# Keys and values of the memory: from the second block's layers to the first block, by way of DRAM

## The reference

```python
def mixer_layer(x, mem, layer_idx, g_norm, w_in, lam_p, w_mem_kv, g_mem, ...):
    h = rmsnorm(x, g_norm)
    z = jnp.einsum('bsd,dn->bsn', h, w_in)            # w_in: 1024 x 13312
    ...
    mem_n = rmsnorm(mem, g_mem)
    kv = jnp.einsum('bmd,dn->bmn', mem_n, w_mem_kv).reshape(B, mem.shape[1], 2, MEM_HEADS, MEM_HEAD_DIM)
    o_m = memory_attention(mq, kv[:, :, 0], kv[:, :, 1])
    ...
    return x + jnp.einsum('bsd,de->bse', merged, w_out)

def second_block(x, mem, ...):
    for l in range(DEPTH):                            # DEPTH = 2
        x = mixer_layer(x, mem, l, g_norm[l], w_in[l], ..., w_mem_kv[l], g_mem[l], ...)
    return rmsnorm(x, g_final)
```

## Time and profile before

| | us |
|---|---|
| median of 3 runs | 2410.48 |
| lowest, highest | 2403.91, 2410.59 |
| profiled execution, its own time | 2403.4 |
| its span | 2401.7 |
| PE busy | 2059.7 (86%) |
| VectorE, ScalarE, POOL busy | 480.6, 377.8, 14.3 |
| moved by DMA | 588.20 MB, 245 GB/s over the span |

### The profile page before, as it was taken

One profiled execution on the slowest core, in us unless ns is written; L12 is line 12 of the kernel. 1 busy time (PEld: TensorE's weight loads), 2 busy tenths in 40 slices (PEclk: granted clock), 3 DMA queues, 4 the chain that ended last, 5 costly groups with the idle time before them and its releaser, 6 DMA issues.

```text
span 2401.7 us, 35672 instructions
## 1 busy us (share of the span) xinstructions
PE 2059.7 (86%) x15302; PEld 1405.7 (59%) x15302; DVE 480.6 (20%) x970; ACT 377.8 (16%) x840; POOL 14.3 (1%) x21
## 2 busy tenths in 40 slices
PE   7868988878738998888739999999985999999997
PEld 4636666666536666666527487455543848745543
DVE  3531111111251111111220023221211002222112
ACT  2501111001011110000020122221102012221111
POOL 0000000000000000000000000000000000000000
PEclk9878999989978998899969999999997999999999
DMA  9156999999976999999754433523315443353330
GB/s 355 49 219 239 421 421 420 420 419 420 394 305 246 420 420 420 420 420 420 310 189 166 149 120 126 189 86 128 140 38 209 140 166 115 106 192 105 123 123 26
DMA packets 140628, 588.20 MB, mean 245 GB/s; under 512 B 13680, under 2 KB 14960, under 8 KB 90928
## 3 DMA queue, kind: packets, MB, share of 16 engines
q1 hardware_dynamic: 134368, 565.13, 59.7%
q0 software_dynamic: 6096, 20.72, 2.4%
HBM read 579.51 MB, written 6.29 MB: 244 GB/s over the span
## 4 chain that ended last, share of the span: by engine, by line
issue 52%; PE 40%; DVE 4%; ACT 2%; DMA 1%; DVEq 0%; SPq 0%; POOL 0%; ACTq 0%; POOLq 0%
PE ps L441 22%; PE ps L430 10%; PE ps L387 2%; PE ps L436 2%; PE ps L413 2%; PE ps L359 1%; ACT arena L507 1%; DVE arena L632 1%; DVE tiny L636 1%; DVE arena L656 1%; DMA arena<-in_mem_dram 1%; ACT arena L491 1%; DVE arena L655 0%; DMA pos_i<-in_positions_dram 0%; DMA arena<-in_diff_lambda_dram 0%
## 5 line engine op out<-in xcount | busy, mean ns | idle before, releaser
L441 PE MATMUL ps<-ring,xT 128*128 128x512 f32 x960 | 418.3, 593 | 0.0
L925 PE MATMUL ps<-ring,xT 128*32 128x128 f32 x8192 | 278.4, 293 | 87.7 <-DMA ring<-in_moe_w_dram 80.6
L925 PEld LDWEIGHTS ps<-ring,xT 128*32 128x32 f32 x8192 | 251.4, 115 | 140.3 <-DMA ring<-in_moe_w_dram 87.1
L430 PE MATMUL ps<-xT,ring 128*128 128x256 f32 x1408 | 309.7, 380 | 0.0
L441 PEld LDWEIGHTS ps<-ring,xT 128*128 128x128 f32 x960 | 180.7, 190 | 214.4 <-issue 213.7
L430 PEld LDWEIGHTS ps<-xT,ring 128*128 128x128 f32 x1408 | 265.4, 190 | 39.9 <-issue 4.9
L907 PE MATMUL ps<-arena,x_tm 128*128 128x128 f32 x1024 | 257.4, 410 | 9.8 <-DVE arena L1433 8.5
L907 PEld LDWEIGHTS ps<-arena,x_tm 128*128 128x128 f32 x1024 | 248.9, 334 | 18.6 <-issue 9.7
L958 PE MATMUL ps<-arena 128*32 128x512 f32 x768 | 141.9, 700 | 31.7 <-DVE arena L1448 31.7
L441 PE MATMUL ps<-ring,arena 128*128 128x512 f32 x320 | 141.5, 599 | 1.8 <-ACT arena L491 1.8
L359 PE MATMUL ps<-consts,arena 128*128 128x128 f32 x352 | 56.3, 299 | 86.4 <-DVEq L618 70.7
(11 more groups left out here) (239 smaller groups left out, 1448.5 us busy)
## 6 DMA issues: line engine op xcount, KB each, us to landing
ring<-in_moe_w_dram SPq DMA_DIRECT2D x288, 1024.0 KB, 24.4
ring<-in_w_in_dram SPq DMA_DIRECT2D x52, 2048.0 KB, 8.2
arena<-in_moe_w_dram SPq DMA_DIRECT2D x96, 1024.0 KB, 26.1
ring<-in_w_mem_kv_dram SPq DMA_DIRECT2D x4, 2048.0 KB, 9.3
ring<-in_w_br_diff_dram SPq DMA_DIRECT2D x4, 2048.0 KB, 7.9
ring<-in_w_out_dram SPq DMA_DIRECT2D x4, 2048.0 KB, 8.0
ring<-gap_bias POOLq DMA_DIRECT2D x4, 1536.0 KB, 10.1
gap_bias<-arena POOLq DMA_DIRECT2D x1, 5120.0 KB, 53.5
```

Source lines behind the costliest of these rows:

```text
L430: m = nc.tensor.matmul(bank[:, u * T:(u + 1) * T], w[:, k, f * P:(f + 1) * P], x_[:, k, :], start=(k == 0), stop=(k == KD - 1))
L441: m = nc.tensor.matmul(bank, x_[:, k, half * P:(half + 1) * P], w[:, k, :], start=(k == 0), stop=(k == KD - 1))
L925: m = nc.tensor.matmul(ps[SL * q:SL * q + SL, g % 2, s * P:(s + 1) * P], xs[:, g % 2, k, s * SL:(s + 1) * SL], w[:, c0:c0 + 2 * P - 1:2], ...
```

## The change

The keys and values of the memory no longer are made in the second block. In the first block:

- SP loads `mem` and both layers' `g_mem` at the start, and the memory's weights of layer 0 (4 MB) into slots 0 and 1, where experts 0 and 1 were loaded before; expert 0 is loaded after the second keys piece, expert 1 after the last values piece, expert 2 when both stores are done.
- ScalarE squares `mem`, VectorE scales it by the root, PE turns it, VectorE copies it to `memT`. POOL multiplies it by `g_mem` of layer 0 and of layer 1 and stores the second product in DRAM (`memT_dram`).
- PE makes the keys in two pieces (`mem_keys`, 16 matmuls of 256 columns each) and the values in two (`mem_values`, 8 of 512 columns each). Layer 0: keys before attention, keys and values after the output product, values behind the logits. Layer 1: both keys pieces ahead of the pooling products, with `memT` read back, values behind these, values behind the logits.
- ScalarE (VectorE for the very first) copies each piece to SBUF, and POOL stores keys and values in `mk_dram` and `mv_dram`.
- Around the pooling layer SP loads the memory's weights of layer 1 and expert 0, then the pooling's vectors, and experts 1 to 3 at later points. The scaling of `acc` by ScalarE moves ahead of the exponentials.

In the second block the two chunks, the squares, scaling, turns and copies of `mem` are gone, and POOL reads keys and values back behind `g_norm`. The diff, cut to its core:

```diff
-    plan = [(("mem_kv", 0), None, None), (("mem_kv", 1), None, None)]
-    plan += [(w[c], None, None) for c in range(8)]
+    plan = [(w[c], None, None) for c in range(8)]
...
+        mem_tm, memT = places(ring, 2 * UPW, 3 * UPW, (TT, D), (KD, T))
+        mem_sq = carve(arena, 8448, TT, D)
+        memT_of = [carve(ring, 2 * UPW, KD, T), carve(ring, 3 * UPW, KD, T)]
+        mk_w = [carve(ring, 0, KD, CW), carve(ring, UPW, KD, CW)]
+        mv_w = [carve(ring, UPW, KD, CW), carve(ring, 2 * UPW, KD, CW)]
+        mk_new = [carve(ring, s * UPW + KD * T, MH, T) for s in (2, 3)]
+        mv_new = [carve(ring, s * UPW + KD * T + MH * T, TT, MH * HD) for s in (2, 3)]
...
-                for src in (mem_tm, h_tm):
-                    turn_tiles([[src[:, t, k::KD] for k in (2 * c, 2 * c + 1) for t in range(TT)] for c in range(4)])
-                pe.wait_ge(sem("turn_read"), l * NTURN + 8)
+                turn_tiles([[h_tm[:, t, k::KD] for k in (2 * c, 2 * c + 1) for t in range(TT)] for c in range(4)])
+                pe.wait_ge(sem("turn_read"), l * NTURN + 4)
...
-                for n, src in enumerate((x_tm, mem_tm)):
-                    for t in range(TT):
-                        i = nc.scalar.activation(PT3.rearrange("p a b -> p (a b)")[:, 0:D], src[:, t, :], ACT.Square,
-                                                 accum_out=ssq4[:, 2 * n + t:2 * n + t + 1])
-                        i.then_inc(sem("ssq_each"), 1)
-                        act.wait_ge(sem("ssq_each"), l * 4 + 2 * n + t + 1)
+                for t in range(TT):
+                    i = nc.scalar.activation(PT3.rearrange("p a b -> p (a b)")[:, 0:D], x_tm[:, t, :], ACT.Square,
+                                             accum_out=ssq4[:, t:t + 1])
+                    i.then_inc(sem("ssq_each"), 1)
+                    act.wait_ge(sem("ssq_each"), l * TT + t + 1)
                 act.sem_inc(sem("ssq_ready2"), 1)
-                act_root2(act, l * 2 + 1, 4)
+                act_root2(act, l * 2 + 1, TT)
...
-                    pool.dma_start(mem_tm, a["mem"][0].rearrange("(t p) d -> p t d", p=P)).then_inc(sem("mem_in"), 16)
                     pool.dma_start(g_x, a["g_norm"][bass.ds(l, 1), :].rearrange("a d -> (a d)").partition_broadcast(P)
                                    ).then_inc(sem("g_in"), 16)
-                    pool.dma_start(g_m, a["g_mem"][bass.ds(l, 1), :].rearrange("a d -> (a d)").partition_broadcast(P)
-                                   ).then_inc(sem("g_in"), 16)
+                    pool.dma_start(mkT, mk_dram[bass.ds(l, 1)].rearrange("a p (h t) -> (a p) h t", h=MH)).then_inc(
+                        sem("mkv_in"), 16)
+                    pool.dma_start(mv, mv_dram[bass.ds(l, 1)].rearrange("a p (t n) -> (a p) t n", t=TT)).then_inc(
+                        sem("mkv_in"), 16)
...
+            sp.dma_start(mem_tm, a["mem"][0].rearrange("(t p) d -> p t d", p=P)).then_inc(sem("mem_in"), 16)
+            sp.dma_start(gm, a["g_mem"].rearrange("l (p k) -> p l k", k=KD), allow_slow_non_contiguous=True).then_inc(
+                sem("gm_in"), 16)
             sp.dma_start(wuq, a["mla_w_uq"][0].rearrange("(k p) n -> p k n", p=P)).then_inc(sem("wuq_in"), 16)
             sp.dma_start(wukv, a["mla_w_ukv"][0]).then_inc(sem("wukv_in"), 16)
             sp.dma_start(wo, a["mla_w_o"][0].rearrange("(k p) n -> p k n", p=P)).then_inc(sem("wo_in"), 16)
-            for e in range(3):
-                load_up(sp, 0, e)
+            load_mem_w(sp, 0)
...
+            sp.wait_ge(sem("mkv_ps"), 2)
+            load_up(sp, 0, 0)
             sp.wait_ge(sem("ln_done"), 1)
             load_ln(sp, 0, 1, gain, shift)
+            sp.wait_ge(sem("mkv_ps"), 4)
+            load_up(sp, 0, 1)
             sp.wait_ge(sem("A_ready"), 1)
             load_route(sp, 1)
+            sp.wait_ge(sem("mk_out"), 16)
+            sp.wait_ge(sem("mv_out"), 16)
+            load_up(sp, 0, 2)
             load_experts(sp, 0, 0)
...
+            sp.wait_ge(sem("up"), done * NE + NE - 1)
+            load_mem_w(sp, 1)
+            sp.wait_ge(sem("up"), done * NE + NE)
+            sp.wait_ge(sem("memT_out"), 16)
+            sp.dma_start(memT_of[1], memT_dram.rearrange("p (k t) -> p k t", k=KD)).then_inc(sem("memT_in"), 16)
+            load_up(sp, 1, 0)
             sp.wait_ge(sem("down"), done * (2 * GROUPS) + 2 * GROUPS - 2)
             for dst_, src_ in ((pb, a["pool_b"]), (psc, a["pool_scale"])):
                 sp.dma_start(dst_, src_[0].partition_broadcast(P)).then_inc(sem("pool_in"), 16)
             load_ln(sp, 1, 0, pool_gain, pool_shift)
-            for e in range(4):
-                sp.wait_ge(sem("up"), done * NE + NE - 3 + e)
-                load_up(sp, 1, e)
             sp.wait_ge(sem("down"), nsw * (2 * GROUPS))
             for e in range(6):
                 load_down(sp, 1, e)
+            sp.wait_ge(sem("mkv_ps"), 6)
+            load_up(sp, 1, 1)
             sp.wait_ge(sem("ln_done"), 2)
             load_ln(sp, 1, 1, gain, shift)
             sp.wait_ge(sem("ln_done"), 3)
             load_up(sp, 1, 4)
             load_down(sp, 1, 6)
             load_down(sp, 1, 7)
+            sp.wait_ge(sem("mkv_ps"), 8)
+            load_up(sp, 1, 2)
+            sp.wait_ge(sem("mk_out"), 32)
+            sp.wait_ge(sem("mv_out"), 32)
+            load_up(sp, 1, 3)
             load_experts(sp, 1, nsw)
...
+        def mem_keys(pe, layer, half, bank):
+            if half == 0:
+                pe.wait_ge(sem(f"mkv_w0"), 16 * (layer + 1))
+            for u in range(2):
+                f = 2 * half + u
+                for k in range(KD):
+                    i = nc.tensor.matmul(ps[:, bank, u * T:(u + 1) * T], mk_w[layer][:, k, f * P:(f + 1) * P],
+                                         memT_of[layer][:, k, :], start=(k == 0), stop=(k == KD - 1))
+            i.then_inc(sem("mkv_ps"), 1)
+
+        def mem_values(pe, layer, half, bank):
+            if half == 0:
+                pe.wait_ge(sem(f"mkv_w1"), 16 * (layer + 1))
+            for k in range(KD):
+                i = nc.tensor.matmul(ps[:, bank, :], memT_of[layer][:, k, half * P:(half + 1) * P],
+                                     mv_w[layer][:, k, :], start=(k == 0), stop=(k == KD - 1))
+            i.then_inc(sem("mkv_ps"), 1)
+
         def transpose_x(pe, n):
 
+            if n == 1:
+                pe.wait_ge(sem("mkv_taken"), 3)
+            if n == 3:
+                pe.wait_ge(sem("mkv_taken"), 7)
...
+            mem_values(pe, layer, 1, 3)
             pe.wait_ge(sem("A_ready"), layer + 1)
...
+            pe.wait_ge(sem("mem_normed"), 1)
+            for c in range(4):
+                for u in range(2):
+                    for t in range(TT):
+                        i = nc.tensor.transpose(ps[:, 4 + c, u * T + t * P:u * T + (t + 1) * P],
+                                                mem_tm[:, t, 2 * c + u::KD], ident)
+                i.then_inc(sem("memT_ps"), 1)
...
+            pe.wait_ge(sem("k_ready"), 8)
+            pe.wait_ge(sem("memT0_ready"), 1)
+            mem_keys(pe, 0, 0, 3)
...
+            pe.wait_ge(sem("mkv_taken"), 1)
+            mem_keys(pe, 0, 1, 6)
+            mem_values(pe, 0, 0, 7)
...
+            pe.wait_ge(sem("memT_in"), 16)
+            for half in range(2):
+                mem_keys(pe, 1, half, half)
...
+            pe.wait_ge(sem("pool_ready"), 4)
+            mem_values(pe, 1, 0, 7)
...
+            act.wait_ge(sem("ln_done"), 2 * layer + 1)
+            nc.scalar.mul(acc, x_tm, ALPHA).then_inc(sem("acc_begun"), 1)
             act.wait_ge(sem("g_centred"), layer + 1)
             nc.scalar.activation(goh_e, geq, ACT.Exp).then_inc(sem("g_exp"), 1)
+            take_mem(act, layer, 3, 3)
             act.wait_ge(sem("e_gap"), layer + 1)
             nc.scalar.activation(rat, tx, ACT.Exp).then_inc(sem("e_exp"), 1)
-            act.wait_ge(sem("ln_done"), 2 * layer + 1)
-            nc.scalar.mul(acc, x_tm, ALPHA).then_inc(sem("acc_begun"), 1)
...
+            v.wait_ge(sem("ssq_mem"), 1)
+            ch(nc.vector.tensor_scalar(ssqm, ssqm, 1.0 / D, None, ALU.mult))
+            inverse_root(v, ch, ssqm, TT, 1e-6)
+            for t in range(TT):
+                ch(nc.vector.tensor_scalar(mem_tm[:, t, :], mem_tm[:, t, :], ssqm[:, t:t + 1], None, ALU.mult))
+            v.sem_inc(sem("mem_normed"), 1)
...
+            v.wait_ge(sem("memT_out"), 16)
+            v.wait_ge(sem("mkv_ps"), 1)
+            nc.vector.tensor_copy(mk_new[0][:, 0:2, :], ps[:, 3, :].rearrange("p (a b) -> p a b", a=2)).then_inc(
+                sem("mkv_taken"), 1)
             v.wait_ge(sem("gap_out"), 16)
...
+            pool.wait_ge(sem("gm_in"), 16)
+            pool.wait_ge(sem("memT_taken"), 4)
+            nc.gpsimd.tensor_tensor(memT_of[0], memT, over(gm[:, 0, :], 2, T), ALU.mult).then_inc(sem("memT0_ready"), 1)
+            pool.wait_ge(sem("memT0_ready"), 1)
```

(13 more changed lines are left out.)

88 lines of the change are left out of this document (57 added, 31 removed).

## The result

The changed kernel took 2334.1 us (median of 4 runs, 2328.7 to 2338.1), the kernel before 2407.2 in the same session (4 runs, 2403.7 to 2410.6): ratio 0.970, 95% interval 0.968 to 0.972, some 73 us less. The profiled execution took 2332.05 us, its span is 2330.4, 71.3 under the 2401.7 of before. The forecast was 2327, between the 2324 and the 2331 that its 79 us less gave from the profiled execution and from the median.

The account below looks back on a forecast made before the run. Expert layers were taken as bound by DMA bytes, the second block by PE, with seams between. -83.5 - 2 - 3 + 6.4 + 3 = -79 us gave 2324 from the profile, 2331 from the median; forecast 2327, range 2309 to 2347.

Parts of the forecast that it names:

- the first mask after 73: Sign of being wrong, at attention's start in the first block: first mask starting after 73 us; about 70.7 was expected.
- a wait for expert 2: Sign of being wrong, in the expert layers: PE waits for the weights of experts 2 or 3.
- The removal: Second block's two layer entries: 12.8 to 15.7 us remain of 53.9 and 58.0; 39.5 and 44 go, -83.5 us.
- Before attention: First block, layer 0's first keys piece ahead of scores: mask 2.1 late, then made up by a warmer clock; -2 us (-3 to +3).
- GpSimd's products: POOL's multiplications of memT by g_mem before attention: 2.6 to 26 us each, taken nearest 2.6, with 26 us free; cost nothing.
- Rival (b): Before attention: POOL's products or memT's store hold VectorE's first mask, +8 to +18 us, 2335 to 2345; chance 0.08.
- Rival (c): Before attention: VectorE's rope waits while POOL multiplies, up to one product, 2.6 to 5 us, 2330; chance 0.04.
- First LayerNorm and routing: Layer 0 after attention: keys and values pieces keep PE warm, logits 3.3 and transposes 0.4 us shorter; -3 us, +4 if cold.
- Step to the pooling: After layer 0's last combine: memT lands near E + 5, both keys pieces delay the pooling products; +6.4 us (4 to 11).
- Routing of layer 1: Behind the pooling: logits or last values piece may run cold after some 13 us of idleness; 0 to +10, taken +3 us.
- Stores: Keys' and values' stores, awaited before expert 2 (layer 0) or 3 (layer 1) loads: each may take 10 us for nothing.
- Rival (e): Expert loads wait behind the stores; each us beyond 10 costs one per layer, 2407 at 50 us a store; chance 0.03.

Follow-up runs that it names:

- second_only: Kernel before with only the change's second-block hunks, memory keys and values not made but same-size rows of mem loaded: 2312.2 us, ratio 0.9635.

## Why the prediction was right, and where it was off

The saving came out 6 us under the forecast's 79, but two of the signs by which the text would be wrong were met: the first mask after 73, and a wait for expert 2. So the number is better than the account of where it comes from.

- **The removal** (-83.5): right in mechanism, 4 us small. In the profile -87.1, in the run with the second block's part alone 88. 12.2 us remain after GpSimd's issue of 12.8 to 15.7 forecast; g_norm landed in 4.8 us, so the allowance for 8.3 and for a cold restart was not needed.
- **Before attention** (-2; wrong if the first mask is after 73): this step failed. The text counted the bytes beside memT's store ("SP moves 1 MB less beside it") and never asked when the first half of w_mem_kv lands. That half is queued behind w_o, in rows of 2 KB, and landed at 68.3, 7.6 us after TensorE was ready; the mask came at 78.76. The forecast priced the wait for memT's store, GpSimd's products and the piece itself, and with the weights first all three are hidden (mask at 68.50). The price was +10 at the mask, and 6 to 8 us of time: the last output product ends at 153.6, 153.7 and 153.8 in three profiles with the late weights, at 145.6, 148.8 and 146.9 in three with the early ones. The hope that the piece keeps TensorE warm was not borne out: even with the early weights the clock was 0.60 to 0.70 from 70 to 80 us, against 0.50 and 0.83 in the two profiles without the piece.
- **GpSimd's products**: 3.60 us each, nearest to VectorE's row as taken. Rival (b) had the right size and the right place (+8 to +18, first mask), with the wrong cause. The Trainium skill's 4.5 us for an add of that size (GPSIMD Engine Reference, 3.1 Elementwise — side-by-side cycle accounting) is of the same order; the trace's 3.60 decides.
- **Rival (c)**, a lock between VectorE and GpSimd: never put to the test. GpSimd was done at 41.1 and rope began at 47.0, with passes of 0.44 as before.
- **First LayerNorm and routing** (-3): transposes 2.06, logits 3.79 and the values piece under VectorE's chain are as said. -5.3 was read, but the same code differs by more, and the unchanged code of second_only has its logits warm there too. That the change earns these 3 us is thus not shown.
- **Step to the pooling** (+6.4): mis-sized by 6 in the profile of the changed kernel. memT landed at E+10.0, not E+5; its load took 17.7 us, behind 4 MB of w_mem_kv. The keys then took 16.8 us where 15.6 was said. The range given (4 to 11) ended short of +12.5. In three more profiles with the same code there memT came at E+6.4, 6.0 and 9.2 and the step cost 8 to 11 us, inside the range: the order and the mechanism were right, the size was 1 to 6 us low.
- **Routing of layer 1** (+3 of 0 to 10): +5.3. The logits were cold after the pause of 13.7 us, 3.3 of it, as the text had considered; but it took the warm 3.79 of the earlier trace rows as given, and second_only shows the same code cold. Moving the keys behind the pooling took the price of both steps away, 11 us by ratio.
- **Stores** (10 us free each): too generous in layer 0, where 0.19 us of wait was already there. Rival (e)'s mechanism is real: 4.1 us later gave 3.47 of wait. How long a store would have to be for the gain to go was not tried.
- Two errors of opposite sign: 4 us more removed, 11 to 12 more paid. That is how 2327 came out near 2334; that they partly cancel is luck.

## What to carry to other kernels

When a product is moved forward to where its engine is idle, ask first when its operand lands: its place in the queue, the size of its contiguous rows, and which queues run beside it, not only its bytes. Work that is to fill a pause belongs inside it: behind the product whose result the other engines then work on, not ahead of that product. Here the keys of layer 1, moved behind the pooling products, cost nothing that can be told, and TensorE came to the logits without a pause. And before reading differences of up to 8 us off two profiles, look at what the same code does in a second one.

## What the runs showed of the hardware

- With the same two stores on another queue beside it, one load of 4 MB in rows of 32 KB landed at 58.3 us, and 2 MB in rows of 2 KB, issued at the same 10.4 us, at 68.3. From 47 to 56 us the queue with the short rows moved 0.56 MB, with the long ones 2.30 MB.
- A 1 MB store took 23 to 30 us to land beside full queues (27.0 in the changed kernel), 0.5 MB about 9 in the routings, and 3.8 when repeated at once in layer 0, with fewer loads beside it (157 GB/s in all, against 317).
- Two profiles with identical code up to the first expert product had it 8.2 us apart, with TensorE's clock at 0.50 or 0.83 from 70 to 80 us.
